# w_out's product as seven half-size products in a row, ple's product behind them

## The chip, the cores and the metric

The kernel runs on one core of a Trainium2 chip. The metric is the device time of one execution in microseconds; the kernel before takes 885.83 us (median of 3 runs, 885.14 to 887.33). TensorE (PE) multiplies matrices, VectorE (DVE) and ScalarE (ACT) work elementwise and can read PSUM, GpSimd (POOL) works elementwise on SBUF, and SyncE (SP) only issues DMAs.

## The reference

Three layers over 512 tokens of width 1024, all in float32. The first one is where the change lies:

```
h = rms_norm(x, pre_norm_gain);  q, k, v, z_a, b, c, u, z_c = split(h @ w_in)      # 512 columns each
attn = rms_norm(diff_attention(q, k, v), subln_gain) * 0.8 * silu(z_a)
conv_out = b * causal_conv(c * u) * silu(z_c)
mixed = concat([attn, conv_out]) @ w_out                        # (512 x 1024) @ (1024 x 1024)
x = x + rms_norm(mixed, post_norm_gain)                         # "m1" is mixed, "x1" the new x
e = rms_norm(p @ w_ple_proj, ple_norm_gain)                     # 256 -> 1024
x = x + sigmoid(x @ w_ple_gate) * e                             # "x2"
```

A gated MLP layer (its product `v4` with a_w_in_2 is also computed in seven half-size products before the change) and a layer of windowed attention follow; the change does not touch what they compute.

## The kernel before

**Exact products.** Every operand of a large product is split into a high part `hi` (a float32r copy) and a remainder `lo` (value minus `hi`), and each 128x128 by 128x512 step is three matmuls, hi x hi, hi x lo and lo x hi (`exact`, L2073, whose three lines are L2076 to L2078).

**Weights.** They come in units of 1 MB, in the order of `weight_units` (L31). SyncE loads each as two halves into a room (A and B are the two halves of `raw`, G is `gain[1]` and `gain[2]`, K is `tok`). GpSimd splits the units in `SPLIT` (`split_half`, L820): for each half two copies (L841) and two remainders (L850) of 512 columns. The units in `BY_TWO` (L67) are split by ScalarE (copies of 1024 columns, L1118) and VectorE (remainders, L1667). The split values lie in two slots (`whi`, `wlo`) used in turn, so a unit is split only when the unit before the previous one has been used up on TensorE (`SLOT_BEFORE`).

**w_out before.** Four units (column half x row half), each used by four blocks ("T") of a row tile, 12 matmuls a block. Results stay in the eight PSUM banks. The first blocks do three of their four steps ahead ("Th"), while the fourth head of attention is still being finished.

**Seven products before.** For `v4` the 2x2 blocks of activations and weights are combined so that seven products of half size stand for eight. The weight sums are made by DMAs that add into the room, issued by GpSimd (`add_load`, L885); the activation sums by VectorE (`act_sum`, L1669), ScalarE (`sum_hi`) and VectorE again (`act_sum_lo`). Each product is two blocks ("S") of 12 matmuls into two banks; ScalarE keeps the first product (`keep_v4`), VectorE adds the others to it in SBUF (`combine`, L1686).

**Behind w_out.** ScalarE squares each bank (`square`, L940), GpSimd turns the sum of squares into 1/rms (`root`, L783: lines L795 and L798), VectorE scales, applies the gain and adds to `resid` (`post`, L1612: two operations of L1618 that read PSUM, and L1622). TensorE then transposes x1 ("tr x1", L2173), ScalarE copies it (`turned`, L961), VectorE makes the remainder (`rest`, L1421), and the gate's product reads it. ple's product fills the time in between; ScalarE copies and squares its result directly from PSUM (`ple_out`, L1068). `gate` needs units split by GpSimd.

**Order.** All engines run queues in program order. TensorE's is written out in `tensor_order` (L188), each block waiting for its data (`ready`) and for its bank (`emptied`, L557). GpSimd's is the order of units; the dictionary `after` (L881 and on) says which roots, masks and DMAs stand behind which half: a key ending in -0.5 is a place between a half's copies and its remainders, -0.25 one between its two remainders. SyncE's is the order of units with `late` calls ahead of some of them.

Of the kernel before, what the change touches and what calls it, by code (L numbers as in the profile page):

```python
# [9 lines left out]
S = 512  # L10
# [20 lines left out]
def weight_units():  # L31
# [13 lines left out]
    u += [("wo", 2 * c + kh, "T", "w_out", 4 * kh, 512 * c) for c in range(2) for kh in range(2)]  # L45
# [21 lines left out]
BY_TWO = [n for n, u in enumerate(UNITS) if u[2] == "S" or u[:2] in (("z4", 0), ("z4", 4))]  # L67
# [13 lines left out]
ROOMS = {("v4", 0): "BAG", ("v4", 1): "GAB"}  # L81
# [3 lines left out]
OPERAND7 = (0, 1, 4, 3, 6, 5, 7)  # L85

# [14 lines left out]
def room_of(n):  # L101

    s, j = UNITS[n][:2]
    if s == "a":
        return ROOM_A[j]
    if s == "k5":
        return "K"
    k = WHOLE[n] if n < UNIT_NO["v5", 0] else WHOLE[n] + (s == "v5")
    return "AB"[k % 2]


def previous_in_room():

    last, before = {}, {}
    for n, (s, j, kind, *_) in enumerate(UNITS):
        if s == "v4":
            continue
# [11 lines left out]
def landings():  # L129
# [7 lines left out]
    for n, (s, j, kind, *_) in enumerate(UNITS):  # L137
# [8 lines left out]
        if s == "v4" and j % 7 == 0:  # L146
# [36 lines left out]
HEADS = {("v", 0, 0, t): 2 for t in range(T)} | {("wo", 0, 0, t): 3 for t in range(T)}  # L183
# [4 lines left out]
def tensor_order():  # L188
# [32 lines left out]
    turn = lambda name, t: [("tr", name, t, j) for j in range(2)]  # L221
# [32 lines left out]
def bank_of(b):  # L254

    kind = b[0]
    if kind == "tr":
        name, t, j = b[1:]
        return {"x": (2 * t + j) % 3, "p": 4 + j, "x1": t + 4 * j, "h": (2 * t + j) % 4,
# [20 lines left out]
    if kind == "s4":  # L280
        return 4 * (b[1] // 2 % 2) + b[1] % 2
    return {"gn": lambda c: (7, 3)[c], "warm": lambda n: 6, "sc": lambda i, m: 4 + m, "tw": lambda i: 6, "pv": lambda i: 7, "ta": lambda h: IN_TURN.index((h,)) % 4,
            "ple": lambda t, c: t + 4 * c, "wt": lambda j: 4 + j, "rw": lambda j: 6 + j,
# [35 lines left out]
def program(nc, x, p, pre_norm_gain, w_in, lambda_q1, lambda_k1, lambda_q2, lambda_k2, subln_gain,  # L319
# [9 lines left out]
    with ctx:  # L329
# [79 lines left out]
        e_sb = lambda t: big[:, t, 0:D]  # L409
        wsr = gcv[:, :, :].rearrange("p a b -> p (a b)")[:, 0:NG * P]  # L410
# [74 lines left out]
        def of_product(s, q, h):  # L485
# [9 lines left out]
                 "wo": (actB_hi, actB_lo), "gate": (actA_hi, actA_lo),  # L495
# [61 lines left out]
        def emptied(b):  # L557
# [16 lines left out]
            if kind == "T":  # L574
                s, c, _, t = b[1:]
                return {"v": (v_copied, t + 1), "wo": (post_scaled, 2 * t + c + 1),
                        "gate": (gate_tanh, 4 * c + t + 1),
                        "f": (f_gained, 4 * c + t + 1)}[s]
            if kind == "S":
                _, q, r = b[1:]  # L580
                g = q // 7
# [3 lines left out]
            if kind == "A":  # L585
                n, r = b[1:]
                product = UNITS_A[n][0]
                if product == 0:
                    return x7_kept, 4 + r + 1
                return c7_made, 28 + {3: 1 + r, 1: 3 + r, 4: 6 + 4 * r, 2: 8 + 4 * r, 5: 13 + r, 6: 15 + r}[product]  # L590
# [3 lines left out]
            if kind == "t5":  # L594
# [3 lines left out]
                    "ple": (squared["e"], 2 * a + b[-1] + 1), "wt": (wct_copied, a + 1),  # L598
# [3 lines left out]
        def last_block(n):  # L602
# [8 lines left out]
            if kind == "S":  # L611
                return BLOCK["S", s, j, 1] if s == "v4" else BLOCK["A", j, 1]
# [6 lines left out]
        def _(sp):  # L619
# [7 lines left out]
            def load_half(n):  # L627
# [3 lines left out]
                if (s, j) == ("z4", 0):  # L631
                    sp.wait_ge(w7_lo, 2 * 10 + h + 1)
                elif (s, j) == ("u4", 0):
                    sp.wait_ge(w7_lo, 2 * 12 + h + 1)
# [8 lines left out]
            def load_a(n):  # L643

                u = UNIT_NO["a", n]
                for h in range(2):
                    if n in (1, 3):
                        sp.wait_ge(w7_lo, 2 * 13 + 2)
# [7 lines left out]
            def load7(s, g, nth, h):  # L656

                dst, src, landed = quarter7(s, g, nth, h)
                sp.dma_start(dst, src).then_inc(landed, 16)

            def loads_v4():
# [12 lines left out]
                for h in range(2):  # L674
                    sp.wait_ge(w7_lo, 2 * 1 + h + 1)
                    load7("v4", 0, 5, h)
                for h in range(2):
                    sp.wait_ge(w7_lo, 2 * 3 + h + 1)
# [1709 lines left out]
```

## Time and profile before

| | |
|---|---|
| median of 3 runs | 885.83 us |
| profiled execution | 885.75 us |
| its span | 884.0 us |
| TensorE busy in the span | 868.2 us (98%), granted clock 0.998 |
| VectorE, ScalarE, GpSimd busy | 537.2, 360.3, 542.8 us |
| HBM read | 99.79 MB |

Times in the rows are microseconds from the start of the span unless marked ns. A busy TensorE only says that matmuls were in flight; its pace is the distance between starts. Idle time of an engine that is not the bottleneck costs nothing.

### The profile page before, as it was taken

To read this page: it belongs to the slowest core of one execution; us is meant where nothing else is said; L and a number is where in the kernel's file an instruction comes from. 1 tells how busy PE (TensorE), PEld (TensorE's weight loads), DVE (VectorE), ACT (ScalarE), POOL (GpSimd) and SP (SyncE) were. 2 spreads that over 40 slices of the span, in tenths; PEclk is the share of its full clock that TensorE was granted. 3 is DMA by queue.
4 is the path that set the end of the run, shared out by engine and by line. 5 is a ranking of instruction groups with operands and counts; after the bars stand their busy time and mean duration, and the time that the engine had idled before them with its cause. 6 is when DMAs were issued, how large, how long until landed. Compare 5 with 4: busy or idle time off the path is not lost.

```text
span 884.0 us, 11936 instructions
## 1 busy us (share of the span) xinstructions
PE 868.2 (98%) x4220; PEld 722.0 (82%) x4220; DVE 537.2 (61%) x880; ACT 360.3 (41%) x804; POOL 542.8 (61%) x604
## 2 busy tenths in 40 slices
PE   8999999999999999999999999999997999999997
PEld 6888888888888787888888888888887888888886
DVE  6125648875035489775765535556996457788624
ACT  4123333431134377546112321113775536767622
POOL 7766556587789832317975038771359798566352
PEclk9999999999999999999999999999999999999999
DMA  7533231342322468885742253526962222112202
GB/s 198 167 120 96 74 92 51 96 143 92 128 90 96 124 146 177 208 203 190 162 124 95 73 190 96 125 90 152 217 180 71 72 73 93 51 49 72 73 1 95
DMA packets 81517, 102.65 MB, mean 116 GB/s; under 512 B 11826, under 2 KB 54322, under 8 KB 81459
## 3 DMA queue, kind: packets, MB, share of 16 engines
q1 hardware_dynamic: 72752, 85.12, 30.1%
q0 software_dynamic: 8704, 16.78, 11.2%
q8 instruction: 34, 0.56, 0.3%
q14 instruction: 25, 0.20, 0.1%
q10 hardware_dynamic: 2, 0.00, 0.0%
HBM read 99.79 MB, written 2.10 MB: 115 GB/s over the span
## 4 chain that ended last, share of the span: by engine, by line
PE 88%; POOL 4%; DVE 2%; DMA 2%; ACT 2%; issue 1%; POOLq 0%; DVEq 0%; ACTq 0%
PE bank L2076 26%; PE bank L2078 26%; PE bank L2077 26%; PE bank L2319 2%; PE bank L2347 1%; PE bank L2173 1%; DMA gain<-in_a_w_in 1%; DVE wlo L1667 1%; POOL wlo L850 1%; PE bank L2292 1%; PE bank L2342 1%; PE bank L2341 1%; DMA raw<-in_a_w_in 1%; POOL ms L795 1%; POOL whi L841 1%
## 5 line engine op out<-in xcount | busy, mean ns | idle before, releaser
L850 POOL TENSOR_TENSOR wlo<-raw,whi 128x512 fp32r<-128x512 f32 x204 | 280.4, 1404 | 0.7 <-ACT whi L972 0.7
L841 POOL TENSOR_SCALAR whi<-raw 128x512 fp32r<-128x512 f32 x202 | 140.8, 733 | 188.1 <-PE bank L2078 179.1
L2076 PE MATMUL bank<-actB_hi,whi 128*128 128x512 f32 (+1 forms) x416 | 159.6, 384 | 0.6 <-POOL wlo L850 0.6
L2077 PE MATMUL bank<-actB_lo,whi 128*128 128x512 f32 (+1 forms) x416 | 158.7, 381 | 0.0
L2078 PE MATMUL bank<-actB_hi,wlo 128*128 128x512 f32 (+1 forms) x416 | 158.5, 381 | 0.0
L2076 PE MATMUL bank<-whi,actA_hi 128*128 128x512 f32 x318 | 125.9, 396 | 1.2 <-DVE actA_lo L1421 0.7
L2078 PE MATMUL bank<-whi,actA_lo 128*128 128x512 f32 x318 | 124.0, 390 | 0.0
L2077 PE MATMUL bank<-wlo,actA_hi 128*128 128x512 f32 x318 | 123.9, 390 | 0.0
L2076 PEld LDWEIGHTS bank<-actB_hi,whi 128*128 128x128 f32 x416 | 78.3, 188 | 15.4 <-issue 1.1
L2078 PEld LDWEIGHTS bank<-actB_hi,wlo 128*128 128x128 f32 x416 | 78.2, 188 | 15.2
L2077 PEld LDWEIGHTS bank<-actB_lo,whi 128*128 128x128 f32 x416 | 78.3, 188 | 14.1
L2076 PE MATMUL bank<-actA_hi,whi 128*128 128x512 f32 x224 | 87.9, 392 | 0.0
L2077 PE MATMUL bank<-actA_lo,whi 128*128 128x512 f32 x224 | 87.4, 390 | 0.0
L2078 PE MATMUL bank<-actA_hi,wlo 128*128 128x512 f32 x224 | 87.3, 390 | 0.0
L2076 PEld LDWEIGHTS bank<-whi,actA_hi 128*128 128x128 f32 x318 | 59.7, 188 | 15.3 <-issue 1.9
L2078 PEld LDWEIGHTS bank<-whi,actA_lo 128*128 128x128 f32 x318 | 59.7, 188 | 12.6
L2077 PEld LDWEIGHTS bank<-wlo,actA_hi 128*128 128x128 f32 x318 | 59.8, 188 | 12.0 <-issue 0.2
L2076 PE MATMUL bank<-whi,actB_hi 128*128 128x512 f32 x144 | 56.5, 393 | 0.2 <-DVE wlo L1667 0.2
L2078 PE MATMUL bank<-whi,actB_lo 128*128 128x512 f32 x144 | 56.1, 390 | 0.0
L2077 PE MATMUL bank<-wlo,actB_hi 128*128 128x512 f32 x144 | 56.0, 389 | 0.0
L1776 DVE TENSOR_TENSOR acc<-acc,gcv 128x512 f32<-128x512 f32 x16 | 15.6, 974 | 58.3 <-ACT gcv L1228 58.3
L2078 PEld LDWEIGHTS bank<-actA_hi,wlo 128*128 128x128 f32 x224 | 42.1, 188 | 8.9
(269 smaller groups left out, 1579.4 us busy)
## 6 DMA issues: line engine op xcount, KB each, us to landing
raw<-in_a_w_in SPq DMA_DIRECT2D x44, 512.0 KB, 4.2
raw<-in_w_in SPq DMA_DIRECT2D x32, 512.0 KB, 3.9
raw<-in_b_w_in SPq DMA_DIRECT2D x16, 512.0 KB, 3.4
raw<-in_a_w_out SPq DMA_DIRECT2D x12, 512.0 KB, 3.3
gain<-in_a_w_out POOLq DMA_DIRECT2D x9, 512.0 KB, 8.2
raw<-in_w_out SPq DMA_DIRECT2D x8, 512.0 KB, 3.4
raw<-in_w_ple_gate SPq DMA_DIRECT2D x8, 512.0 KB, 3.3
gain<-in_a_w_in POOLq DMA_DIRECT2D x8, 512.0 KB, 7.7
```

What stands on the lines that cost most here:

```text
L795: pool.tensor_scalar(m, ss[:, n, t, 0:1], ss[:, n, t, 1:2], EPS, ALU.add, ALU.add).then_inc(ms_ready, 1)
L841: pool.tensor_scalar(H, src[:, i * HALF:(i + 1) * HALF], 1.0, 1.0, ALU.mult, ALU.mult).then_inc(w_hi, 1)
L850: ins = pool.tensor_tensor(L, src[:, i * HALF:(i + 1) * HALF], H.bitcast(f32), ALU.subtract)
L1667: V.tensor_tensor(L, src, H.bitcast(f32), ALU.subtract).then_inc(w7_lo, 1)
L1776: V.tensor_tensor(acc[:, f % 2, :], acc[:, f % 2, :], gcv[:, f % 2, 0:S], ALU.mult).then_inc(zu_made, 1)
L2076: M(out_, whi_, xhi_, start=start, stop=False)
L2077: M(out_, whi_, xlo_, start=False, stop=False)
L2078: return M(out_, wlo_, xhi_, start=False, stop=stop)
L2173: ins = nc.tensor.transpose(bank[:, k * P:(k + 1) * P], src, ident[:, :])
L2292: ins = M(bank[:, qt * P:(qt + 1) * P], wgtT1[:, k * P:(k + 1) * P], tile(vtok, k)[:, h * P:(h + 1) * P], start=k == 0, stop=k == qt)
L2319: ins = M(bank[:, n * P:(n + 1) * P], big[:, n, f * P:(f + 1) * P], wcT[:, (f // 2) * P:(f // 2 + 1) * P], start=True, stop=True)
L2341: M(out_, q, khi(g)[:, keys], start=True, stop=False)
```

## The change

- w_out becomes seven units (`wo`, 0 to 6) of kind "S". Units 0 to 4 and 6, and ple's unit, go to ScalarE and VectorE; unit 5 stays with GpSimd. The rooms are A, B and G; ple's weights go to K (`tok`), loaded once the attention no longer needs it.
- SyncE loads the quarters of w_out (`loads_wo`, `loads_late_wo`), and the gains' load moves behind unit 3, since they lie in G. GpSimd issues the adding DMAs: one behind `b 1`, three in a row behind `zc 1`, each waiting for the remainders of the product that used the room before.
- The conv result is written to `zaT` (float32) so that it can be summed; it waits for the attention head of the same number.
- The seven results are summed in `big` by `keep_7` and `combine`; m1's squares and `post` read them there. ple's result goes to another part of `big` (`e_raw`).
- On TensorE: products 0 to 3, p's turned tiles, products 4 to 6, ple's first three row tiles, x1's tile 0, ple's last, x1's tile 1, and then gate blocks and x1's tiles in turn.
- m1's four roots move from around ple's unit into the split of gate's first unit. ple's squares stand behind the turned x1 tiles on ScalarE and read SBUF.

```diff
-    u += [("wo", 2 * c + kh, "T", "w_out", 4 * kh, 512 * c) for c in range(2) for kh in range(2)]
+    u += [("wo", q, "S", "w_out", 0, 0) for q in range(7)]
...
-BY_TWO = [n for n, u in enumerate(UNITS) if u[2] == "S" or u[:2] in (("z4", 0), ("z4", 4))]
+BY_TWO = [n for n, u in enumerate(UNITS) if u[2] == "S" and u[:2] != ("wo", 5)
+          or u[:2] in (("ple", 0), ("z4", 0), ("z4", 4))]
...
+ROOMS = {("wo", 0): "ABG", ("v4", 0): "BAG", ("v4", 1): "GAB"}
...
-    o += [("Th", "wo", 0, 0, t) for t in range(T)] + [("tr", "p", 0, k) for k in range(2)]
-    o += [("T", "wo", 0, 0, t) for t in range(T)]
-    o += [("T", "wo", 0, 1, t) for t in range(T)]
-    o += [("T", "wo", 1, kh, t) for kh in range(2) for t in range(T)]
-    for t in range(T):
-        o += [("ple", t, c) for c in range(2)]
-        if t:
-            o += [("tr", "x1", t - 1, j) for j in range(2)]
-    o += [("T", "gate", 0, 0, 0)] + [("tr", "x1", 3, j) for j in range(2)]
-    o += [("T", "gate", 0, 0, t) for t in range(1, T)] + [("wt", j) for j in range(2)]
+    o += [("S", "wo", q, r) for q in range(4) for r in range(2)] + [("tr", "p", 0, k) for k in range(2)]
+    o += [("S", "wo", q, r) for q in (4, 5, 6) for r in range(2)] + [("ple", t, c) for t in range(3) for c in range(2)]
+    turn = lambda name, t: [("tr", name, t, j) for j in range(2)]
+    o += turn("x1", 0) + [("ple", 3, c) for c in range(2)] + turn("x1", 1) + [("T", "gate", 0, 0, 0)]
+    o += turn("x1", 2) + [("T", "gate", 0, 0, 1)] + turn("x1", 3) + [("T", "gate", 0, 0, t) for t in (2, 3)]
+    o += [("wt", j) for j in range(2)]
...
-            after[at("ple", 0, 0)] = [lambda: root("m1", 0, D)]
-            after[at("ple", 0, 1)] = [lambda t=t: root("m1", t, D) for t in range(1, T)]
+            after[at("gate", 0, 0) - 0.25] = [lambda: root("m1", 0, D)]
+            after[at("gate", 0, 0)] = [lambda: root("m1", 1, D)]
+            after[at("gate", 0, 1) - 0.5] = [lambda: root("m1", 2, D)]
+            after[at("gate", 0, 1) - 0.25] = [lambda: root("m1", 3, D)]
...
+            after[at("b", 1, 1)] = [lambda: add_load("wo", 0, 3)]
+            after[at("zc", 1, 1)] += [lambda n=n: add_load("wo", 0, n) for n in (4, 6, 7)]
...
+            hi_7("wo", 2)
+            sum_hi(0, "wo")
+            for r in range(2):
+                keep_7("wo", 0, r)
+            hi_7("wo", 3)
+            sum_hi(1, "wo")
+            hi_7("wo", 4)
+            sum_hi(2, "wo")
+            for k in range(2):
+                turned("p", 0, k)
+            sum_hi(3, "wo")
+            for t in range(2):
+                square_m1(t, 0)
+            hi_7("wo", 6)
+            hi_two(UNIT_NO["ple", 0])
+            ple_out(0)
+            for t in range(2):
+                square_m1(2 + t, 1)
+            for t in range(2):
+                square_m1(t, 1)
+            ple_out(1)
+            for t in range(2):
+                square_m1(2 + t, 0)
+            ple_out(2)
             for j in range(2):
-                turned("x1", 3, j)
+                turned("x1", 0, j)
+            ple_out(3)
+            square_e(0)
+            for t in range(1, T):
+                for j in range(2):
+                    turned("x1", t, j)
+                square_e(t)
...
-                    V.scalar_tensor_tensor(acc[:, c, :], psum[t + 4 * c][:, :], rstd[:, NORMS[name], t:t + 1],
+                    V.scalar_tensor_tensor(acc[:, c, :], out_wo(t, c), rstd[:, NORMS[name], t:t + 1],
...
+            out_of = lambda *a: combine(0, *a, s="wo")
+            act_sum(0, "wo")
+            lo_7("wo", 2)
+            act_sum_lo(0, "wo")
+            act_sum(1, "wo")
+            lo_7("wo", 3)
+            act_sum_lo(1, "wo")
+            act_sum(2, "wo")
+            out_of(1, (0, 0), (2, 0), ALU.add, 0)
+            lo_7("wo", 4)
+            act_sum_lo(2, "wo")
+            act_sum(3, "wo")
             for k in range(2):
                 rest("p", 0, k)
+            act_sum_lo(3, "wo")
+            out_of(4, (2, 0), (2, 0), ALU.add, 0)
+            lo_7("wo", 6)
+            out_of(2, (0, 1), (2, 0), ALU.subtract, 3)
+            out_of(3, (2, 0), (2, 0), ALU.add, 3)
+            for h in range(2):
+                lo_two(UNIT_NO["ple", 0], h)
+            out_of(2, (2, 1), (2, 0), ALU.subtract, 7)
+            out_of(5, (0, 1), (0, 1), ALU.add, 5)
+            out_of(6, (2, 0), (2, 0), ALU.add, 7)
             dve.wait_ge(gain_in[1], 16)
+            post("m1", post_scaled, 0, 1, x1_ready)
+            post("m1", post_scaled, 1, 1, x1_ready)
+            for t in range(2):
+                for j in range(2):
+                    rest("x1", t, j)
+                post("m1", post_scaled, 2 + t, 1, x1_ready)
+            for t in range(2, T):
                 for j in range(2):
                     rest("x1", t, j)
```

## Rows read from the trace of the kernel before

**Rows 1.** The page's head, its busy engines and its slices of the granted clock.

```profile
span 884.0 us, 11936 instructions
...
PE 868.2 (98%) x4220; PEld 722.0 (82%) x4220; DVE 537.2 (61%) x880; ACT 360.3 (41%) x804; POOL 542.8 (61%) x604
...
PEclk9999999999999999999999999999999999999999
```

**Rows 2.** The page's chain of waits, its shares by engine.

```profile
PE 88%; POOL 4%; DVE 2%; DMA 2%; ACT 2%; issue 1%; POOLq 0%; DVEq 0%; ACTq 0%
```

**Rows 3.** Windows view, w_out's stage: busy us (instructions) of PE, PEld, DVE, ACT, POOL.

```profile
223.80:259.10 35.30, 35.30 (x158) 29.19 (x157) 4.36 (x6) 5.54 (x16) 24.88 (x28) 1.00 0.31 105
```

**Rows 4.** Timeline of TensorE: start us, length us, engine, line, operation, operands, count.

```profile
223.59 0.47 PE L2076 MATMUL bank<-whi,actB_hi 128*128 128x512 f32 x1
...
259.07 0.39 PE L2076 MATMUL bank<-whi,actA_hi 128*128 128x512 f32 x1
...
271.78 1.03 PE L2173 MATMUL bank<-ident,resid 128*128 128x128 f32 x8
```

**Rows 5.** Timeline of ScalarE at the start of w_out's product.

```profile
214.83 0.60 ACT L1020 ACTIVATE th<-bank 128x512 f32<-128x512 f32 x1 [3.99 <-PE bank L2078]
```

**Rows 6.** Timeline of VectorE, the last convolution tile.

```profile
216.19 1.79 DVE L1541 TENSOR_TENSOR acc<-acc,gcv 128x512 f32<-128x512 f32 x1
```

**Rows 7.** Timeline of ScalarE, a weight copy and a square from SBUF.

```profile
340.31 1.06 ACT L1118 ACTIVATE whi<-raw 128x1024 fp32r<-128x1024 f32 x1 [1.53 <-PE bank L2078]
...
296.68 0.63 ACT L950 ACTIVATE junk<-resid 128x512 f32<-128x512 f32 x1 [1.03 <-DVE resid L1653]
```

**Rows 8.** Timeline of VectorE: a remainder, two combinations, the addition in `post`.

```profile
338.99 1.22 DVE L1667 TENSOR_TENSOR wlo<-gain,whi 128x1024 fp32r<-128x1024 f32 x1
340.12 1.28 DVE L1696 TENSOR_TENSOR big<-bank,big 128x512 f32<-128x512 f32 x2
...
260.50 1.23 DVE L1622 TENSOR_TENSOR resid<-resid,acc 128x1024 f32<-128x1024 f32 x1
```

**Rows 9.** GpSimd's adding DMAs by line: duration ns min/median/max, and their landing.

```profile
L894 POOL DMA_DIRECT2D raw<-in_a_w_in x8: 1186/1218/1792, 311.7 to 363.5; - x8
...
DMA to landing us min/median/max: 6.1/7.7/14.9
```

**Rows 10.** Timeline of GpSimd, an undisturbed half of a w_out unit.

```profile
226.76 1.20 POOL L841 TENSOR_SCALAR whi<-raw 128x512 fp32r<-128x512 f32 x2 [3.10 <-PE bank L2078]
227.93 2.54 POOL L850 TENSOR_TENSOR wlo<-raw,whi 128x512 fp32r<-128x512 f32 x2
```

**Rows 11.** Timeline of GpSimd and VectorE where they meet, single instructions.

```profile
194.97 1.70 POOL L850 TENSOR_TENSOR wlo<-raw,whi 128x512 fp32r<-128x512 f32 x1
195.57 1.65 DVE L1530 SCALAR_TENSOR_TENSOR acc<-gcv,convc,acc 128x512 f32<-128x512 f32 x1
196.64 1.74 POOL L850 TENSOR_TENSOR wlo<-raw,whi 128x512 fp32r<-128x512 f32 x1
...
281.11 1.37 POOL L795 TENSOR_SCALAR ms<-ss 128x1 f32<-128x1 f32 x1
281.11 1.28 DVE L1639 SCALAR_TENSOR_TENSOR big<-big,rstd,gain 128x1024 f32<-128x1024 f32 x1 [3.16 <-POOL rstd L798]
...
262.49 0.74 DVE L1618 SCALAR_TENSOR_TENSOR acc<-bank,rstd,gain 128x512 f32<-128x512 f32 x1
```

**Rows 12.** Timeline of GpSimd: a root of m1; the mask behind gate's first unit.

```profile
252.32 0.30 POOL L795 TENSOR_SCALAR ms<-ss 128x1 f32<-128x1 f32 x1
252.71 0.58 POOL L798 TENSOR_TENSOR rstd<-ms,mhalf 128x1 f32<-128x1 f32 x1
...
271.50 1.10 POOL L856 TENSOR_SCALAR_AFFINE_SELECT gcv<-gcv 128x1024 f32<-128x1024 f32 x1
```

**Rows 13.** Timeline of GpSimd, gate's fourth unit and the idle time before it.

```profile
298.34 1.16 POOL L841 TENSOR_SCALAR whi<-raw 128x512 fp32r<-128x512 f32 x1 [2.24 <-PE bank L2078]
```

**Rows 14.** Timeline of TensorE, the longest gap behind the start.

```profile
668.46 0.74 PE L2173 MATMUL bank<-ident,big 128*128 128x128 f32 x5 [1.72 <-ACT big L1304]
```

More of the change, by code:

```diff
@@ L105, in room_of @@
         return ROOM_A[j]
-    if s == "k5":
+    if s in ("k5", "ple"):
         return "K"
@@ L115, in previous_in_room @@
     for n, (s, j, kind, *_) in enumerate(UNITS):
-        if s == "v4":
+        if kind == "S" and s != "a":
             continue
@@ L180 @@
 BANKS_F = ((1, 2, 0, 4), (5, 3, 6, 7))
-HEADS = {("v", 0, 0, t): 2 for t in range(T)} | {("wo", 0, 0, t): 3 for t in range(T)}
+HEADS = {("v", 0, 0, t): 2 for t in range(T)}
 HEADS |= {("gate", 1, 1, 3): 2}
@@ L630, in load_half @@
                 s, j, kind, name, k0, c0 = UNITS[u]
[L631 to L634, printed above, removed]
+                after = {("gate", 0): ("wo", 5), ("gate", 1): ("wo", 6), ("z4", 0): ("v4", 10), ("u4", 0): ("v4", 12)}
+                if s == "ple":
+                    sp.wait_ge(pe_block, BLOCK["pv", 15])
+                elif (s, j) in after:
+                    room_free(UNIT_NO[after[s, j]], h)
                 elif ROOM_BEFORE[u] is not None:
@@ L659, in load7, with loads_wo, loads_late_wo @@
                 sp.dma_start(dst, src).then_inc(landed, 16)
+            def loads_wo():
+                for h in range(2):
+                    load7("wo", 0, 2, h)
+                for nth, before in ((0, ("b", 1)), (1, ("zc", 1))):
+                    for h in range(2):
+                        room_free(UNIT_NO[before], h)
+                        load7("wo", 0, nth, h)
+            def loads_late_wo():
+                for h in range(2):
+                    room_free(UNIT_NO["wo", 1], h)
+                    load7("wo", 0, 5, h)
+                ws_load()
+                for h in range(2):
+                    room_free(UNIT_NO["wo", 3], h)
+                gain_loads()
+                bs_load()
             def loads_v4():
@@ new lines, in act_sum @@
+            def act_sum(i, s="v4"):
+                upper, lower = slice(0, S // 2), slice(S // 2, S)
+                one, two = feature(s, 0), feature(s, 1)
+                a11, a12, a21, a22 = one[:, :, upper], two[:, :, upper], one[:, :, lower], two[:, :, lower]
+                if i:
+                    dve.wait_ge(s7_lo, SUMS7[s] + i)
+                elif s == "v4":
+                    dve.wait_ge(h_copied, 2 * T)
+                else:
+                    dve.wait_ge(lo["attn"], NH1)
+                    dve.wait_ge(lo["conv"], 4)
+                place, first, second, op = ((a22, a21, a22, ALU.subtract), (a21, a11, a21, ALU.subtract),
+                                            (a22, a22, a11, ALU.subtract), (a22, a12, a22, ALU.add))[i]
+                V.tensor_tensor(place, first, second, op).then_inc(s7_made, 1)
@@ new lines, in act_sum_lo, with combine @@
+            def act_sum_lo(i, s="v4"):
+                dve.wait_ge(s7_hi, SUMS7[s] + i + 1)
+                V.tensor_tensor(s7(actA_lo, i), feature(s, 1 - (i == 1))[:, :, S // 2:S], s7(actA_hi, i).bitcast(f32),
+                                ALU.subtract).then_inc(s7_lo, 1)
+            def combine(g, m, place, other, op, waits, s="v4", rows=range(2)):
+                for r in rows:
+                    t, c = place
+                    u, d = other
+                    b = ("S", s, 7 * g + m, r)
+                    dve.wait_ge(pe_block, BLOCK[b])
+                    if waits:
+                        dve.wait_ge(c7_made, 14 * GROUP7[s, g] + waits + r)
+                    else:
+                        dve.wait_ge(x7_kept, 2 * GROUP7[s, g] + r + 1)
+                    V.tensor_tensor(out7(s, g, t + r, c), psum[bank_of(b)][:, :], out7(s, g, u + r, d), op)\
+                        .then_inc(c7_made, 1)
@@ L2203, in ready @@
                         pe.wait_ge(lo["x"], 2 * t + 1 + kh)
-                    if s == "wo":
-                        pe.wait_ge(*((lo["attn"], NH1 - (kind == "Th")) if kh == 0 else (lo["conv"], 4)))
                     if s == "gate":
```

250 lines of the change are left out of this document (117 added, 133 removed).

## The prediction

> **What bounds the kernel now.** I read the head of the page first: TensorE is busy 868.2 of 884.0 us, at a granted clock of 9 tenths or more in every slice [rows 1]. The chain of waits says the same of the end: 88% of it is TensorE [rows 2]. Then the stage of the change in a windows view: from 223.8 to 259.1 us TensorE is busy all 35.30 us, at full clock, while VectorE works 4.36 us, ScalarE 5.54 and GpSimd 24.88 [rows 3]. So w_out's product is bound by TensorE's own stream. Its pace comes from the timeline: the first matmul behind p's turned tiles is at about 223.67 and ple's first at 259.07, with 156 matmuls between, 0.227 us each; a pair of turned tiles (8 transposes, the one of 271.78) holds it for 0.87 us, so that the gate's first block begins at 272.65 [rows 4]. The last product before w_out ends at about 214.7, where ScalarE takes it up at 214.83 [rows 5]. I use that as the start.
>
> Two things follow. A removed matmul is worth 0.227 us of the span, and any wait put before TensorE costs its full length. There is next to nothing to absorb it: the gate that follows runs back to back.
>
> **What the change removes.** Before: 4 units x 4 row tiles x 4 k x 3 = 192 matmuls. After: 7 products x 2 row tiles x 4 x 3 = 168. 24 x 0.227 = **-5.4 us**. The ple and gate matmuls and the turned tiles are the same in number.
>
> **What the first products wait for.** All four heads of attention must now be split at the start, where three did. VectorE's last attention split is at 212 us, ahead of 214.7; no cost. The second product needs the last convolution tile. Its product ran for 1.79 us beside GpSimd [rows 6]; with GpSimd idle I take 0.7, as for other operations of 512 columns. Two splits of a w_out unit now stand ahead of it on VectorE. ScalarE: tanh and conv copy (0.6 each, [rows 5]) and two copies of 1024 columns (about 1.0 each, [rows 7]) end at 217.9, then the last conv copy 218.5. VectorE splits the second unit to 219.85 (1.13 a half, [rows 8]) and the conv tile to 220.5. TensorE wants it at 214.7 + 5.44 = 220.2: **+0.4 us**.
>
> **Products 2 to 4.** Each costs ScalarE two weight copies and a sum's copy (3 us), VectorE two weight remainders, a sum and its remainder (4 x 1.15 = 4.6 us), against 5.44 us of TensorE. My table, in the frame of before: sum 0 ready 225.1 (wanted 226.05), sum 1 230.8 (231.5), sum 2 236.8 (237.85). The adding DMAs land 6.1 to 14.9 us after issue, median 7.7 [rows 9]; The one that product 4 needs is issued at 222.8 and 223.9, wanted at 231.5: no wait at the median, up to 4 us at the worst row. I take 0.
>
> **Product 5: GpSimd's unit.** GpSimd stands in the wait for product 4's remainders (235.6), issues two DMAs (1.2 us each, [rows 9]), and may split once product 3 has ended, at 236.95. Undisturbed a half takes 1.2 + 2.5 = 3.7 us [rows 10]: ready at 244.6, wanted at 243.3 + 6 x 0.227 = 244.7. But the trace shows GpSimd and VectorE taking turns, a whole instruction at a time, when VectorE reads two SBUF operands. GpSimd's 194.97 lasts 1.70, VectorE's 195.57 lasts 1.65 where its plain length is 0.75, GpSimd's 196.64 lasts 1.74 for 1.27; and a one-column GpSimd operation at 281.11 took 1.37 beside a VectorE product of 1.28, where 0.30 is usual [rows 11]. A VectorE operation with one operand in PSUM takes no turn: 0.74 at 262.49, in the middle of GpSimd's copies. In these 7.5 us VectorE has three of the first kind: the rest of sum 3 (0.8), its remainder (1.15), the first remainder of unit 6 (1.1). Ready at 247.7: **+3.1 us** (0 if they did not collide).
>
> **Behind the last product: E.** Let E be its end. TensorE then wants x1's tile 0 at E + 36 x 0.227 = 8.2, tile 1 after ple's last two blocks, and the gate's first block at 8.2 + 0.87 + 2.72 + 0.87 = E + 12.7. Before, gate's first unit was complete on GpSimd at 271.50, 1.1 us ahead of the gate's 272.65 [rows 4, 12]. Now three things lengthen this unit, since all four roots of m1 stand inside its split.
> - GpSimd: copies 1.2, remainder 1.27, done at E + 2.7; then root 0 waits for ScalarE's fifth square. ScalarE first copies ple's two blocks (to E + 3.4), then does three squares at 0.63 [rows 7]: E + 5.3. Root: 0.95 [rows 12]. So at E + 6.35 three remainders (3.8), two copies (1.2) and three roots (2.5) are left, 7.5 us.
> - VectorE: `post` used to read PSUM; now it reads `big`, so all three of its operations read two SBUF operands: 0.7 + 0.7 + 1.2 = 2.6 us a tile (the last is 1.23 at 260.50, [rows 8]).
> - Each root releases a `post`, and each `post` takes turns with GpSimd. Between E + 6.35 and the end stand GpSimd's 7.5 us and the `post` of tiles 0, 1 and 2, 7.8 us, in series: 6.35 + 7.5 + 7.8 = E + 21.6. x1's tile 0 is ready at E + 10.9 (wanted 8.2), tile 1 at E + 15.1, both covered by the later wait.
>
> The gate starts at E + 21.6 instead of 12.7: **+8.9 us**, of which the last piece is 5.6 us of TensorE idle. Without collisions x1's tile 0 is ready at 6.8 + 2.6 = E + 9.5 (a wait of 1.3), the gate begins at 9.5 + 4.5 = E + 14: +1.3. I take the colliding value, to which rows 11 are nearest.
>
> **Further on.** From gate 0's end to gate 2's end GpSimd took 271.50 to 296.10 (298.34 less its idle 2.24) = 24.6 us before, and the third unit was wanted at 298.1 [rows 12, 13], 25.5 us after the gate's start at 272.65. Now a whole `post` (2.6) falls into gate 1's split, and one more pair of turned tiles (0.87) lies ahead of that need: 27.2 against 26.3, **+0.9**. ple's squares, moved behind the turned tiles, are ready before their roots (E + 31 against 33): 0. ple's own weights, now in `tok`, are issued at 237.9 and split at E - 2: 0. SP's and the other gains' loads have over 8 us: 0. The last product's combinations (PSUM with SBUF, 0.64 each, [rows 8]) end at E + 1.5, before VectorE is needed.
>
> **Sum.** -5.4 + 0.4 + 3.1 + 8.9 + 0.9 = +7.9. The profiled execution took 885.75 us (span 884.0), 0.08 below the median of 885.83. 885.75 + 7.9 = **893.7 us**.
>
> **A rule against this.** The longest gap on TensorE in the trace, 1.7 us of idle ahead of 668.46, left its granted clock at full [rows 1, 14]. The Trainium skill, "TensorE: Matmul & The Clock Gate", section "Why this matters for your kernels", warns that longer gaps between bursts put the array back to its lower clock. No row here shows a gap of 5.6 us, so the sum does not hold it; by the page the first matmuls behind the gap would run slower.
>
> **Rivals.**
> 1. *The engines hardly collide.* The seven products flow and only the roots' chain is felt: -5.4 + 0.4 + 1.3 = -3.7, 882.1 us. For it: VectorE was idle most of this stage. Against: the turns of [rows 11]. Chance 0.18.
> 2. *They collide by half*, as GpSimd's and VectorE's operations often miss each other: -5.4 + 0.4 + 1.5 + 4 + 0 = +0.5, 886.3 us, between 885 and 889. Chance 0.16, half of it within 0.3%, half slower.
> 3. *The lower clock* in the gap before the gate: the next 24 matmuls and 8 turned tiles (6.3 us at 0.227) at the 1.2 GHz level take double: 893.7 + 6.3 = 900.0. Against: gaps in this trace left the clock alone, but all were shorter. Chance 0.08.
> My forecast, slower by 3 to 12 us: 0.58.
>
> **How the numbers follow.** 0.3% (2.7 us) is about what this kernel's timing can tell from no change. Faster: 0.18. Same: 0.08. Slower: 0.58 + 0.08 + 0.08 = 0.74. The range goes from rival 1 (882.1, most of it in) to 898: the forecast plus 4 us for late adding DMAs. The forecast's own range is 889 to 898.
>
> **What would show it.** Right: TensorE's wait for `wlo` of GpSimd inside product 5 (about 3 us) and before gate's first block (about 5 us, the largest), one of about 2.7 us before x1's tile 0, GpSimd's remainders at 2 us and more in gate's first unit, `post` at about 2 us a pair instead of 1.41. Wrong: the gate starting within 14 us of the last product's end, or 168 matmuls in one unbroken row with the same slack behind them.

## The result and the profile after

The kernel after takes 894.06 us (median of 4 runs, 893.11 to 894.13) against 885.49 us before (median of 4, 884.73 to 887.33): by the means of the runs 1.0091 times as long, 95% interval 1.0074 to 1.0109. The profiled execution took 894.03 us at a span of 891.9, so 7.9 us of span more than before.

The head of the page: TensorE is busy as long as before [rows 1] with 24 matmuls fewer, and the span is longer; the clock row, which averages over 22 us, hides what happened to it.

```profile
span 891.9 us, 11939 instructions
...
PE 867.8 (97%) x4196; PEld 720.1 (81%) x4196; DVE 571.6 (64%) x916; ACT 379.5 (43%) x824; POOL 525.5 (59%) x580
...
PEclk9999999999999999999999999999999999999999
...
PE 84%; POOL 5%; DVE 4%; ACT 2%; DMA 2%; issue 2%; POOLq 0%; DVEq 0%; ACTq 0%
```

The last of these lines is the chain of waits by engine: TensorE has lost four points [rows 2], two of them to VectorE, one to GpSimd. Where, the timeline of TensorE shows (starts as in [rows 4]):

```profile
219.56 0.39 PE L2175 MATMUL bank<-whi,actB_lo 128*128 128x512 f32 x1
220.17 0.47 PE L2173 MATMUL bank<-whi,actB_hi 128*128 128x512 f32 x1 [0.22 <-issue]
...
244.08 0.39 PE L2175 MATMUL bank<-whi,actA_lo 128*128 128x512 f32 x1
246.88 0.67 PE L2173 MATMUL bank<-whi,actA_hi 128*128 128x512 f32 x1 [2.41 <-POOL wlo L876]
247.35 0.63 PE L2174 MATMUL bank<-wlo,actA_hi 128*128 128x512 f32 x1
...
250.63 0.40 PE L2173 MATMUL bank<-whi,actA_hi 128*128 128x512 f32 x1
...
258.12 0.39 PE L2173 MATMUL bank<-whi,actA_hi 128*128 128x512 f32 x1
...
266.06 0.39 PE L2175 MATMUL bank<-whi,actA_lo 128*128 128x512 f32 x1
268.84 1.07 PE L2270 MATMUL bank<-ident,resid 128*128 128x128 f32 x8 [2.40 <-DVE resid L1736]
...
272.52 1.03 PE L2270 MATMUL bank<-ident,resid 128*128 128x128 f32 x8
277.41 0.47 PE L2173 MATMUL bank<-whi,actA_hi 128*128 128x512 f32 x1 [3.85 <-DVE actA_lo L1483]
277.71 0.57 PE L2174 MATMUL bank<-wlo,actA_hi 128*128 128x512 f32 x1
...
281.36 0.39 PE L2174 MATMUL bank<-wlo,actA_hi 128*128 128x512 f32 x1
```

From start to start, less the 0.23 us that a matmul takes anyway (0.87 for a pair of turned tiles), TensorE waits 0.4 us in front of the second product, 2.6 inside product 5, 2.5 before x1's tile 0 and 4.0 before the gate. E, the end of the last product, is 258.12, where ple's first matmul starts. Before the gate the profile names VectorE's remainder of x1's tile 1 (276.05, in VectorE's timeline below), since it ended last, 0.07 us behind GpSimd's. But the gate's first block asks only for tile 0's remainder, done at 273.2, and for the unit, whose last remainder GpSimd ended at 277.26: it waited for GpSimd.

Behind two of these waits matmuls stand 0.43 us apart instead of 0.23. The windows view (behind the stretch and its length TensorE's busy us and instructions; the granted clock is the third figure from the end) tells why:

```profile
246.88:250.34 3.46, 3.46 (x9) 2.69 (x10) 3.18 (x5) 0.25 (x1) 0.00 (x0) 0.53 1.02 356
250.34:253.80 3.46, 3.46 (x16) 2.88 (x15) 0.44 (x1) 0.92 (x1) 0.00 (x0) 0.98 0.73 239
...
268.84:272.40 3.56, 3.56 (x20) 3.08 (x21) 3.53 (x4) 1.69 (x3) 3.38 (x5) 1.00 0.02 8
277.41:281.10 3.69, 3.69 (x10) 2.88 (x11) 3.66 (x3) 0.00 (x0) 3.69 (x4) 0.55 0.42 142
```

The granted clock was at the 1.2 GHz level behind the waits in product 5 and before the gate, not behind the one before x1's tile 0. From 246.88 to 250.63 nine matmul steps took 3.75 us instead of 2.1, from 277.41 to 281.36 ten took 3.95 instead of 2.3: 1.65 and 1.6 us.

GpSimd, from product 5's unit to the end of gate's first unit:

```profile
236.93 1.76 POOL L867 TENSOR_SCALAR whi<-raw 128x512 fp32r<-128x512 f32 x2
238.66 3.54 POOL L876 TENSOR_TENSOR wlo<-raw,whi 128x512 fp32r<-128x512 f32 x2
...
243.34 3.49 POOL L876 TENSOR_TENSOR wlo<-raw,whi 128x512 fp32r<-128x512 f32 x2
...
263.98 0.30 POOL L817 TENSOR_SCALAR ms<-ss 128x1 f32<-128x1 f32 x1 [3.06 <-ACT junk L980]
...
264.92 1.29 POOL L876 TENSOR_TENSOR wlo<-raw,whi 128x512 fp32r<-128x512 f32 x1
...
267.86 2.33 POOL L867 TENSOR_SCALAR whi<-raw 128x512 fp32r<-128x512 f32 x2
...
270.96 1.43 POOL L820 TENSOR_TENSOR rstd<-ms,mhalf 128x1 f32<-128x1 f32 x1
...
275.26 2.00 POOL L876 TENSOR_TENSOR wlo<-raw,whi 128x512 fp32r<-128x512 f32 x1
277.22 1.10 POOL L882 TENSOR_SCALAR_AFFINE_SELECT gcv<-gcv 128x1024 f32<-128x1024 f32 x1
```

A pair of remainders takes 3.49 us instead of 2.54, a pair of copies 2.33 instead of 1.20 [rows 10], a one-column operation 1.43 instead of 0.58 [rows 12]. Across them, VectorE's `post` of tile 0 takes 2.38 us for the two operations that took 0.74 each when they read PSUM [rows 11]; the last line is the remainder of x1's tile 1:

```profile
265.06 2.38 DVE L1732 SCALAR_TENSOR_TENSOR acc<-big,rstd,gain 128x512 f32<-128x512 f32 x2 [5.13 <-POOL rstd L820]
267.47 1.23 DVE L1736 TENSOR_TENSOR resid<-resid,acc 128x1024 f32<-128x1024 f32 x1
...
276.05 1.28 DVE L1483 TENSOR_TENSOR actA_lo<-bank,actA_hi 128x512 fp32r<-128x512 f32 x2
```

And ScalarE's squares ahead of the first root, each with the reading of its sum, 0.8 us from start to start and not 0.63:

```profile
261.54 0.62 ACT L980 ACTIVATE junk<-big 128x512 f32<-128x512 f32 x1
262.06 0.19 ACT L980 ACTIVATION_READ_ACCUMULATOR junk<-big 128x1 f32 x1
262.34 0.63 ACT L980 ACTIVATE junk<-big 128x512 f32<-128x512 f32 x1
```

### The profile page after: what moved, and what is told of

It reads as the page before. It is cut to its first block, busy times and chain, and to the rows that moved or that the text cites. A ratio compares the mean times of both kernels' runs of the same rounds, so it can differ in the third digit from the quotient of the medians.

```text
span 891.9 us, 11939 instructions
## 1 busy us (share of the span) xinstructions
PE 867.8 (97%) x4196; PEld 720.1 (81%) x4196; DVE 571.6 (64%) x916; ACT 379.5 (43%) x824; POOL 525.5 (59%) x580
## 4 chain that ended last, share of the span: by engine, by line
PE 84%; POOL 5%; DVE 4%; ACT 2%; DMA 2%; issue 2%; POOLq 0%; DVEq 0%; ACTq 0%
PE bank L2173 25%; PE bank L2174 25%; PE bank L2175 25%; POOL wlo L876 2%; PE bank L2417 2%; DVE wlo L1651 1%; PE bank L2445 1%; DMA gain<-in_a_w_in 1%; PE bank L2270 1%; POOL whi L867 1%; PE bank L2390 1%; PE bank L2440 1%; PE bank L2439 1%; DMA raw<-in_a_w_in 1%; POOL ms L817 1%
## 5 line engine op out<-in xcount | busy, mean ns | idle before, releaser
L876 POOL TENSOR_TENSOR wlo<-raw,whi 128x512 fp32r<-128x512 f32 x188 | 259.9, 1413 | 0.8 <-ACT whi L1002 0.8
L867 POOL TENSOR_SCALAR whi<-raw 128x512 fp32r<-128x512 f32 x186 | 132.2, 748 | 185.9 <-PE bank L2175 180.3
L2173 PE MATMUL bank<-whi,actA_hi 128*128 128x512 f32 x350 | 139.7, 399 | 7.8 <-DVE actA_lo L1483 4.6
L2174 PE MATMUL bank<-wlo,actA_hi 128*128 128x512 f32 x350 | 137.7, 393 | 0.0
L2175 PE MATMUL bank<-whi,actA_lo 128*128 128x512 f32 x350 | 137.7, 393 | 0.0
L2173 PEld LDWEIGHTS bank<-whi,actA_hi 128*128 128x128 f32 x350 | 66.5, 190 | 24.1 <-DVE actA_lo L1483 5.0
L2175 PEld LDWEIGHTS bank<-whi,actA_lo 128*128 128x128 f32 x350 | 66.5, 190 | 14.2
L2174 PEld LDWEIGHTS bank<-actA_lo,whi 128*128 128x128 f32 x224 | 42.1, 188 | 8.3
L2173 PEld LDWEIGHTS bank<-actA_hi,whi 128*128 128x128 f32 x224 | 42.1, 188 | 8.4
L1651 DVE TENSOR_TENSOR wlo<-raw,whi 128x1024 fp32r<-128x1024 f32 x28 | 33.7, 1230 | 14.7 <-ACT whi L1040 14.7
```

Source lines behind the costliest of these rows:

```text
L867: pool.tensor_scalar(H, src[:, i * HALF:(i + 1) * HALF], 1.0, 1.0, ALU.mult, ALU.mult).then_inc(w_hi, 1)
L876: ins = pool.tensor_tensor(L, src[:, i * HALF:(i + 1) * HALF], H.bitcast(f32), ALU.subtract)
L1651: V.tensor_tensor(L, src, H.bitcast(f32), ALU.subtract).then_inc(w7_lo, 1)
L2173: M(out_, whi_, xhi_, start=start, stop=False)
L2174: M(out_, whi_, xlo_, start=False, stop=False)
L2175: return M(out_, wlo_, xhi_, start=False, stop=stop)
```

## The experiments

Each is the kernel after with an edit, but for "The turns, by themselves", which is the kernel before with one; those behind it build on the first two edits. Times are medians; ratios are of the means, with their 95% interval, against the kernel before, run on the same chip beside it.

### Product 5's unit to ScalarE and VectorE

```diff
-BY_TWO = [n for n, u in enumerate(UNITS) if u[2] == "S" and u[:2] != ("wo", 5)
+BY_TWO = [n for n, u in enumerate(UNITS) if u[2] == "S"
...
             sum_hi(3, "wo")
+            hi_7("wo", 5)
...
             act_sum_lo(3, "wo")
+            lo_7("wo", 5)
```

> The changed kernel, but w_out's unit 5 is split by ScalarE and VectorE like the other six, GpSimd has no part in it. My theory (TensorE stands in product 5 because GpSimd's remainders take turns with VectorE, and the granted clock falls behind that gap): the gap of 2.6 us goes, and with it the slow stretch of about 1.7 us behind it; -4 us against the changed kernel, 890 us. Rival (ScalarE and VectorE are as full as GpSimd, so the wait only changes hands: VectorE's remainders now come 2.3 us later for units 6 and ple): a new gap of 1 to 3 us in product 6 or before ple, 892 to 894 us.

888.89 us, 1.0036 (1.0023 to 1.0048). The wait in product 5 is gone, with its slow matmuls, 4.2 us, and E comes 3.7 us sooner. The total fell by more, 5.2 us: the gate's wait fell to 2.4 us, and the matmuls behind it run at full pace, 3.2 us together. Part of that comes back. x1's tile 0 is waited for as before, 2.6 us, but now the clock falls behind that wait (granted 0.53 from 265.17 to 268.81): a pair of turned tiles and five matmuls are slow, 1.6 us. And gate's third unit is waited for, 1.0 us at 301.0.

### m1's squares ahead of ple's first copy

```diff
-            ple_out(0)
             for t in range(2):
                 square_m1(2 + t, 1)
             for t in range(2):
                 square_m1(t, 1)
+            ple_out(0)
```

> The changed kernel, but on ScalarE the four squares (row tiles 2, 3, 0, 1 of column half 1) stand ahead of ple's first two copies instead of behind them. My theory (root 0 waits for ScalarE's squares, and everything up to the gate hangs on it): root 0 at 2.7 us behind the last product instead of 5.7, the gap before x1's tile 0 (2.6 us) goes, the gate begins 3 us sooner; -3 us, 891 us. Rival (GpSimd's own split with its collisions sets the gate's start, whenever the roots come): the gate's start stays within 1 us, only the first of the two gaps goes, 893 to 894 us.

889.73 us, 1.0040 (1.0027 to 1.0054). Root 0 starts 2.9 us behind E instead of 5.9, and the wait before x1's tile 0 is gone. The gate still waits, 3.7 us, and starts at E + 16.3 instead of 19.3: three microseconds for three, as the chain through the root says. The total fell by 4.3 us; 2.9 of it stand up to the gate, the rest was not traced.

### All four roots behind the split

```diff
-            after[at("gate", 0, 0) - 0.25] = [lambda: root("m1", 0, D)]
-            after[at("gate", 0, 0)] = [lambda: root("m1", 1, D)]
-            after[at("gate", 0, 1) - 0.5] = [lambda: root("m1", 2, D)]
-            after[at("gate", 0, 1) - 0.25] = [lambda: root("m1", 3, D)]
-            after[at("gate", 0, 1)] = [mask_ws]
+            after[at("gate", 0, 1)] = [lambda t=t: root("m1", t, D) for t in range(T)] + [mask_ws]
```

> The changed kernel, but all four roots of m1 stand behind the split of gate's first unit, not inside it. My theory (post and the split take turns): the split ends about 7.7 us behind the last product, the posts then run without it; x1's tile 0 is ready at 11.3 (wanted 8.2), the gate begins at about 15.8 instead of 19.1 us behind the last product; -3 us, and up to 1.5 more if the clock stays up; 889.5 to 891 us. Rival (the squares and VectorE's posts alone set the pace, the split only fills their gaps): x1's tiles come 2 to 3 us later and the gate later with them, 894 to 897 us.

890.95 us, 1.0060 (1.0047 to 1.0073). Undisturbed, the split ends at E + 7.7, and the bound passes to the roots and `post`:

```profile
270.24 1.06 PE L2266 MATMUL bank<-ident,resid 128*128 128x128 f32 x8 [3.41 <-DVE resid L1732]
...
283.12 1.07 PE L2266 MATMUL bank<-ident,resid 128*128 128x128 f32 x8 [1.70 <-DVE resid L1732]
```

The wait moved, and became shorter in sum: 3.6 + 1.9 against 2.5 + 4.0 us. The other 1.6 us of the gain are the clock's: behind both waits the matmuls run at full pace.

### `post` without its gain

The multiplication by `post_norm_gain` is left out, so that `post` is one operation of 1024 columns.

```diff
-                for c in range(2):
-                    V.scalar_tensor_tensor(acc[:, c, :], out_wo(t, c), rstd[:, NORMS[name], t:t + 1],
-                                           gain[:, g, c * HALF:(c + 1) * HALF], ALU.mult, ALU.mult)\
-                        .then_inc(done, 1)
-                dve.wait_ge(done, 2 * t + 2)
-                V.tensor_tensor(resid[:, t], resid[:, t], acc[:, :, :].rearrange("p a b -> p (a b)"), ALU.add)\
+                V.scalar_tensor_tensor(resid[:, t], big[:, 2 * (t // 2), (t % 2) * D:(t % 2 + 1) * D],
+                                       rstd[:, NORMS[name], t:t + 1], resid[:, t], ALU.mult, ALU.add)\
                     .then_inc(ready, 1)
```

> The changed kernel, but post leaves out the multiplication by post_norm_gain, so that one operation of 1024 columns (about 1.3 us, two SBUF operands) stands for the three (2.7 us). My theory (the posts stand in series with GpSimd's split): three posts x 1.4 = 4.1 us less in front of the gate, which begins about 15 us behind the last product; -4 us, 890 us, and up to 1.5 more if the clock stays up. Rival (GpSimd waits for squares and roots, not for VectorE): the gate's start moves by less than 1.5 us, 892.5 to 894 us.

892.92 us, 1.0078 (1.0065 to 1.0092). By its interval this can't be told from the change itself, so the reading rests on the trace. The theory failed, and the rival's number held: with some 4 us of VectorE's work gone from beside it the split ends only 1.6 us sooner after E. x1's tile 0 came early enough to cut its wait from 2.5 to 1.2 us, and TensorE then waited for GpSimd alone:

```profile
276.35 0.76 PE L2169 MATMUL bank<-whi,actA_hi 128*128 128x512 f32 x1 [3.66 <-POOL wlo L876]
```

The rival's reason, that GpSimd does not wait for VectorE, did not hold: behind root 0 the split took 10.7 us where GpSimd's own work is 7.6. It lost 3.1 us beside three of VectorE's operations of 1024 columns; in the change it lost 4.7 beside nine, six of them of 512. So what it loses goes by the turns it meets, and is less than VectorE's work added up. The clock's part did not shrink: 20 matmuls followed at the slow pace, where it was 16.

### Ten matmuls in product 5's wait

```diff
+                    if (s, q, r, k) == ("wo", 5, 0, 2):
+                        pe.wait_ge(*emptied(BEFORE["S", "wo", 5, 1]))
+                        for _ in range(10):
+                            M(psum[bank_of(("S", "wo", 5, 1))][:, :], aH, whi[:, SLOT[n], 0:HALF], start=True, stop=True)
```

> The changed kernel with ten more matmuls of 128x512 (2.3 us, into the bank that product 5's second block will open anyway, their result unused) where TensorE stands idle for 2.6 us in product 5. My theory (the granted clock falls because TensorE stands idle there, and the eight matmuls at 0.43 us behind the gap pay for it): the clock stays up, the eight run at 0.227, -1.6 us, 892.4 us. Rival (the slow matmuls there come from the 350 GB/s that the DMA engines move in the same stretch, or the clock falls for another reason): they stay slow, and the fillers cost up to 2 us themselves, 894 to 896 us.

892.30 us, 1.0064 (1.0052 to 1.0076): work that nobody uses made the kernel 1.8 us faster. The filler ends as the unit comes, and in product 5 the clock stays at full:

```profile
244.69 2.43 PE L2242 MATMUL bank<-whi,actA_hi 128*128 128x512 f32 x10
247.29 0.50 PE L2173 MATMUL bank<-whi,actA_hi 128*128 128x512 f32 x1 [0.17 <-POOL wlo L876]
```

In the windows view:

```profile
245.00:251.00 6.00, 5.83 (x26) 4.52 (x25) 4.21 (x6) 1.06 (x1) 2.24 (x2) 1.00 1.00 360
```

The DMA engines are as busy there as in the change (share 1.00 beside 1.02), so they did not slow those matmuls. Up to E only the clock's part is taken out, and counted from the first product E comes 1.5 us sooner. The total of 1.8 us is not that part alone, for behind E the clock fell at another place:

```profile
267.66 1.32 PE L2274 MATMUL bank<-ident,resid 128*128 128x128 f32 x8 [2.40 <-DVE resid L1736]
268.63 0.78 PE L2173 MATMUL bank<-whi,actA_hi 128*128 128x512 f32 x1
269.21 0.63 PE L2174 MATMUL bank<-wlo,actA_hi 128*128 128x512 f32 x1
```

The wait before x1's tile 0 is the one of the change, but slow matmuls follow it, 1.6 us. The gate's wait fell to 2.5 us with none behind it, and gate's third unit is waited for, 0.9 us.

### The turns, by themselves

In the kernel before, VectorE is idle for 28 us of w_out's stage while GpSimd splits. 24 additions are put there.

```diff
+            for i in range(24):
+                dve.wait_ge(lo["conv"], 4 + i)
+                V.tensor_tensor(acc[:, 0, :], acc[:, 1, :], acc[:, 1, :], ALU.add).then_inc(lo["conv"], 1)
+            dve.wait_ge(lo["conv"], 28)
```

> The kernel before, with 24 added VectorE additions (both operands in SBUF, 128x512, one behind the other) in w_out's stage, where VectorE stood idle some 28 us; their results are not used. This measures the turns of GpSimd and VectorE by itself. Theory (a VectorE operation with two SBUF operands and a GpSimd operation wait for each other, once each a turn): beside the added ones GpSimd's remainders take 1.9 to 2.0 us instead of 1.27 and its copies 1.2 instead of 0.6, and the added ones 1.3 to 1.9 us instead of 0.7; w_out's units, split with 3 us to spare, come up to 3 us late, 0 to +4 us in all. Rival (no turns; what slowed GpSimd in the kernel after was its waits for semaphores alone): lengths as before, and no change in the total.

887.88 us, 1.0016 (1.0007 to 1.0025). The timelines of GpSimd and VectorE:

```profile
226.90 2.15 POOL L841 TENSOR_SCALAR whi<-raw 128x512 fp32r<-128x512 f32 x2 [3.09 <-PE bank L2082]
229.01 3.42 POOL L850 TENSOR_TENSOR wlo<-raw,whi 128x512 fp32r<-128x512 f32 x2
...
225.41 30.02 DVE L1629 TENSOR_TENSOR acc<-acc 128x512 f32<-128x512 f32 x24
```

A copy took 1.07 us instead of 0.60, a remainder 1.71 instead of 1.27, an addition 1.25. The turns are there with nothing else changed, but an operation of 512 columns costs GpSimd's 0.45 us, not the 0.65 that I had expected. 1.7 us of waits for GpSimd's units reached TensorE, at 238.0 and 261.1.

### Two edits together, and two ways to go on

`c0_split_and_squares` has the first two edits, `c1_and_roots_behind` the third as well, `c2_two_roots_inside` the first two with roots 0 and 1 inside the split and 2 and 3 behind it.

> The changed kernel with unit 5 split by ScalarE and VectorE and the four squares ahead of ple's first copies. If the two gaps are independent, their gains of 5.2 and 4.3 us add up: 884.5 us, level with the kernel before. Rival (with unit 5's splits on VectorE and ScalarE, the combinations and squares that stand behind them come later, so that the squares' gain shrinks by 1 to 2 us): 886 us.

> As the kernel with both, and with all four roots behind gate's first unit. My theory: x1's tile 0 then waits for that split again (7.7 us behind the last product plus root and post, 11.3 to 12, wanted at 8.2), which early squares can't help: a gap of 3.5 us comes back, the gate at 16 us behind the last product; 886 us. Rival (the roots inside the split are what costs, early or not): faster than the kernel without this step, 883 us.

> As the kernel with both edits, but roots 2 and 3 stand behind gate's first unit and roots 0 and 1 inside it. My theory: root 0 at 2.7 us behind the last product lets x1's tile 0 come in time, the split is spared two roots and one post and ends at about 13 (wanted 12.7), tile 2 is about 1 us late: in sum -5.4 + 0.4 + 1.5 = -3.5 against the kernel before, 882.3 us. Rival (tiles 2 and 3 become the bound, VectorE's posts standing against gate's second unit): gaps of 2 us and more before them, 885 us.

886.83 us (1.0003, 0.9994 to 1.0013), 887.53 (1.0014, 1.0006 to 1.0023) and 887.92 (1.0022, 1.0011 to 1.0033). The first is level with the kernel before: all of the loss is out, and no gain in. It still waits 3.7 us before the gate and has 6 slow steps and a slow pair of turned tiles behind that, 5.3 us, about what the 24 matmuls are worth. The second has 3.6 us before x1's tile 0 in its place, with 2.9 us of slow work behind. The third keeps the clock and spreads its waits (0.9, 1.7, and 2.3 for gate's third unit); its 12 runs span 4.7 us. All three missed what I had expected, by 2.3, 1.5 and 5.6 us: what is taken from one place of GpSimd's line comes up at the next.

### Filling the wait

On top of the first two edits the turned small weights (`wt`, `rw`, 2.6 us of TensorE) and their copies are moved ahead of the gate, the mask behind GpSimd's adding DMAs.

```diff
-    o += turn("x1", 0) + [("ple", 3, c) for c in range(2)] + turn("x1", 1) + [("T", "gate", 0, 0, 0)]
+    o += turn("x1", 0) + [("wt", j) for j in range(2)] + [("ple", 3, c) for c in range(2)] + turn("x1", 1)
+    o += [("rw", j) for j in range(2)] + [("T", "gate", 0, 0, 0)]
...
```

> The kernel with unit 5 split by ScalarE and VectorE and m1's squares ahead of ple's first copy (c0_split_and_squares, 886.8 us), and in addition: the two small turned weights (wt and rw) are moved from between the gate's blocks to behind x1's tiles 0 and 1, ahead of the gate, and the mask on GpSimd (1.1 us) from behind gate's first unit to behind its adding DMAs. Theory (the wait before the gate is GpSimd's split of gate's first unit, and is worth its length plus the slow matmuls behind it): the moved blocks, 0.9 + 1.7 us, fill 2.6 of the 3.7 us, so the clock stays up and some 1.4 us of slow matmuls go too: about 883 us, faster than before. Rival: ScalarE's four more copies ahead of ple's squares, or GpSimd starting gate's second unit no earlier than it did, give the gain back as a later wait for gate's third unit or for the last turned tiles: 886 to 887.

887.70 us, 1.0017 (1.0008 to 1.0025). The wait before the gate is down to 0.9 us of idle time, and the clock stays at full behind it; but the third unit of the gate, which these blocks used to cover, is now missing:

```profile
297.81 0.47 PE L2177 MATMUL bank<-whi,actA_hi 128*128 128x512 f32 x1 [3.69 <-POOL wlo L875]
```

Four matmuls on, the clock falls there too, 1.7 us. The rival held, by its second half: GpSimd's line from E to the gate's third unit is the bound, and TensorE's order only chooses where the wait shows.

### Gate's first unit off GpSimd

On top of the first two edits:

```diff
+          or u[:2] in (("ple", 0), ("gate", 0), ("z4", 0), ("z4", 4))]
...
-            after[at("gate", 0, 0) - 0.25] = [lambda: root("m1", 0, D)]
...
+            after[at("zc", 1, 1)] += [lambda n=n: add_load("wo", 0, n) for n in (4, 6, 7)] + [mask_ws]
+            after[at("zc", 1, 1)] += [lambda t=t: root("m1", t, D) for t in range(T)]
...
+            hi_two(UNIT_NO["gate", 0])
             ple_out(0)
...
+            for t in range(2):
+                post("m1", post_scaled, t, 1, x1_ready)
+                lo_two(UNIT_NO["gate", 0], t)
```

ScalarE also squares the last two parts of m1 behind x1's turned tile 0, and the four roots, which stood inside the split, now follow one another ahead of gate's second unit.

> The kernel with unit 5 split by ScalarE and VectorE and m1's squares first (c0_split_and_squares, 886.8 us), and in addition gate's first unit is taken from GpSimd: ScalarE makes its two copies of 1024 columns behind m1's four first squares (1.06 us each), VectorE its two remainders (1.2 us each) behind post of tile 0 and of tile 1. GpSimd is left with the mask and the four roots there, and gate's second unit. Theory (what the change costs is GpSimd's line from the end of w_out's product to gate's third unit; VectorE's two-SBUF operations and GpSimd's delay each other): with the unit's 7.4 us off that line the gate starts 13 us behind the last product, no wait before the gate of over 0.6 us, no slow matmuls, third unit in time: 3.7 + 1.3 us less, 882 us, faster than before by 4. Rival: VectorE's line (10.4 us of post, 2.4 of remainders, 1.3 of rest and 1.5 of combinations ahead of the gate, in series 15.6 us from the last product's end) now binds: the gate starts at 15 us or later, 884 to 886.

883.30 us (11 runs, 881.99 to 883.95), 0.9969 (0.9958 to 0.9981): faster than both, and the one version in which the seven products pay. The gain is small, 2.0 us by the medians, but all 11 runs lie below the fastest of the 15 beside them (884.72). The same edit to the kernel before was not run; in its trace TensorE waits nowhere between 223.6 and 312 us, so there is no wait for it to remove. TensorE's timeline and a window from E on:

```profile
267.28 0.47 PE L2173 MATMUL bank<-whi,actA_hi 128*128 128x512 f32 x1
...
275.92 1.06 PE L2270 MATMUL bank<-ident,resid 128*128 128x128 f32 x8 [1.72 <-DVE resid L1734]
```

```profile
254.20:275.50 21.30, 19.63 (x97) 15.86 (x96) 20.59 (x25) 17.21 (x40) 12.46 (x14) 1.00 0.18 62
```

The gate starts at 267.28, 13.1 us behind the last product, without a wait and at full clock, as the theory said (E + 13). What the theory did not see is a wait of 1.9 us before x1's tile 3, at 275.92. The second fence, of the windows view, shows VectorE busy 20.59 of 21.30 us (the third figure with a count): the rival's line binds, only at the last tile instead of before the gate. The turns with gate's second unit, which GpSimd now starts at 268.5, may have a part in it; that was not separated.

## Why the prediction was right, and where it was not

The forecast was 893.7 us, "slower"; 894.06 came. By its own steps:

- **24 matmuls fewer, -5.4**: right. 168 in place of 192, at 0.227 us.
- **The second product waits for the convolution, +0.4**: right (219.56 to 220.17).
- **Product 5, GpSimd's unit, +3.1**: 2.6 measured. The place and the releaser are as said. The turns were priced at VectorE's whole operations, 3.05 us; the pairs of 236.93, 238.66 and 243.34 took 0.6, 1.0 and 0.95 longer than in [rows 10], 2.5 us.
- **The gate at E + 21.6, +8.9**: it started at E + 19.3, so +6.6, as 2.5 before x1's tile 0 (2.7 said), nothing before tile 1 (0.6 follows from its numbers) and 4.0 before the gate (5.6 said). The failing step is "GpSimd's 7.5 us and the `post` of tiles 0, 1 and 2, 7.8 us, in series". From 264.92 to 277.26 GpSimd needed 12.3 us where its own work is 7.6, so the turns cost it some 4.7 us, not 7.8; root 0 was 0.5 later than reckoned, since a square stands 0.8 us from the next. The run without gain shows that the two lines aren't in series: 4 us less work on VectorE gave 1.6.
- **The gate's third unit, +0.9**: nothing. TensorE went from the last block of the gate's second unit to the next without a wait. GpSimd had the third unit ready 26.4 us behind the first, not 27.2, and the slow matmuls at the gate's start had held TensorE back by 1.6 us. Where they were missing (unit 5 to ScalarE and VectorE), this wait came, with 1.0 us.
- **No price for the clock**: wrong, 1.65 + 1.6 = 3.2 us. It was held as rival 3, at 6.3 us behind the gate alone and with a chance of 0.08; it came at two places for half of that. The sentence against it ("gaps in this trace left the clock alone, but all were shorter") was a fair reading of [rows 14], but not of a sum that itself forecast gaps of 3 and 5.6 us. By the rule named there, of the Trainium skill's "TensorE: Matmul & The Clock Gate", section "Why this matters for your kernels", the first matmuls behind such a gap run slower. The trace agrees behind the gate's wait, 0.55 of granted clock after 3.85 us of idle time, and shows more than the page says: 0.53 after 2.41 us in product 5, and full clock after 2.40 us before x1's tile 0.
- **SP's loads, ple's weights, the adding DMAs, ple's squares, 0 each**: no wait of TensorE leads to them.

The measured terms: -5.4 + 0.4 + 2.6 + 1.65 + 2.5 + 4.0 + 1.6 = +7.35. Of the 7.9 us of span, 0.3 more stand in v4's product, which waits 0.7 us at 352.6 where it waited 0.4 at 345.3; the last 0.25 I can't place. So the total came out within 0.4 us by errors that cancel: 0.5 + 2.3 + 0.9 too much for collisions, 3.2 too little for the clock.

That the waits along GpSimd's line and the lower clock behind them, and not the seven products themselves, were the cause is shown by taking them apart: unit 5 elsewhere, -5.2; squares first, -4.3; both, level with before; gate's first unit elsewhere too, 0.9969. That turns with VectorE are a part of that line is shown by the additions in the kernel before and by the lengths in the trace. What is not shown is the size of each turn in the change itself, nor how much of the gate's wait would go if there were none. Making the roots on VectorE, which would take GpSimd out of the chain between the squares and `post`, was not tried.

## What to carry to other kernels

An engine's idle share says nothing of what it costs to use it: moving work to VectorE with both operands in SBUF can hold up the GpSimd operations that run beside it, here by 0.45 us for 512 columns, and that falls on whatever waits for GpSimd. When a change puts a wait in a stream that was unbroken, price the lower clock behind it too, with the same care as the wait, and don't take a slow stretch for gone when one wait is: in two of these runs it came back behind the next. And where one engine's line is the bound, reordering its consumer or its own steps only moves the wait (three of these runs); taking a whole unit off the line removed it.

## What the runs showed of the hardware

- Two waits of TensorE of the same length had different ends: idle 2.41 us in product 5, then the 1.2 GHz level for eight matmuls; idle 2.40 us before x1's tile 0, then full clock. With product 5's wait removed or filled, the same 2.40 us before x1's tile 0 was followed by the slow level (granted 0.53 from 265.17 to 268.81 in the first of these runs). The length of the wait alone doesn't decide; what does, no run here tells.
- The turns are regular. In the run with additions, over the 30.0 us of VectorE's 24, GpSimd's remainders were 0.44 us longer each and its copies 0.44 to 0.47, whatever their own length. The Trainium skill, "SBUF — State Buffer", section "SBUF: two separate sides", calls the shared pair of ports an exclusive lock for the whole of an instruction. The trace agrees in kind; a waiting instruction paid 0.45 us where the other is 0.7 long, so by these lengths they overlap in part.
- A one-column GpSimd operation can pay as much as a long one: 1.43 us at 270.96 instead of 0.58.
- Useless matmuls in a wait made the kernel faster, by 1.8 us of 894, though the clock then fell behind a later wait.
